# Turning memory rows before their norm is known, in a hybrid decoder step

## The reference, cut to what matters

```python
def rms_norm(x, g):
    y = xf * lax.rsqrt(jnp.mean(xf * xf, axis=-1, keepdims=True) + EPS)
    return (y * g.astype(jnp.float32)).astype(x.dtype)

def memory_kv(mem, p):            # mem (1, 256, 1024)
    mn = rms_norm(mem, p["g_mem"])
    mk = (mn @ p["w_mk"]).reshape(Bm, M, N_XHEADS, XHEAD_DIM)   # w_mk (1024, 1024)
    mv = (mn @ p["w_mv"]).reshape(Bm, M, N_XHEADS, XHEAD_DIM)
```

## Time and profile before

| | |
|---|---|
| median of 3 runs | 1738.87 us (1736.15 to 1744.55) |
| profiled execution | 1745.4 us, of which its span is 1743.6 us |
| PE busy | 1692.7 us, 97% |
| DVE, ACT busy | 1112.3 us (64%), 917.5 us (53%) |
| first instruction of PE | at 10.65 us |
| chain that ended last | PE 81%, DVE 6%, ACT 5%, DMA 4%, issue 3% |

### The profile page before, as it was taken

How to read it: one execution, slowest core, us unless ns; L and a number is a source line. 1 busy time by engine, 2 the same in 40 slices (tenths; PEclk the granted TensorE clock), 3 DMA queues, 4 the chain that set the end, 5 groups by cost and what they waited for, 6 DMA issues and landing times.

```text
span 1743.6 us, 29783 instructions
## 1 busy us (share of the span) xinstructions
PE 1692.7 (97%) x11750; PEld 1580.7 (91%) x11750; DVE 1112.3 (64%) x2055; ACT 917.5 (53%) x1675; POOL 2.2 (0%) x12
## 2 busy tenths in 40 slices
PE   7999999989999999999999999999999999999998
PEld 7999999845669999888779999999999999999998
DVE  5489998777665677435367767644676534676533
ACT  7534444755667676555456555444545433555433
POOL 0000000000000000000000000000000000000000
PEclk9999999989999999999999999999999999999999
DMA  8899967486215645443534344444445444445443
GB/s 279 202 246 217 234 176 162 155 313 237 86 56 157 186 145 159 148 131 109 162 117 122 109 131 134 131 134 142 137 135 157 139 137 143 135 134 154 139 138 100
DMA packets 400673, 271.45 MB, mean 156 GB/s; under 512 B 54252, under 2 KB 374882, under 8 KB 399184
## 3 DMA queue, kind: packets, MB, share of 16 engines
q1 hardware_dynamic: 395688, 260.72, 51.9%
q10 hardware_dynamic: 4847, 8.83, 1.5%
HBM read 225.40 MB, written 27.23 MB: 145 GB/s over the span
## 4 chain that ended last, share of the span: by engine, by line
PE 81%; DVE 6%; ACT 5%; DMA 4%; issue 3%; SPq 1%; ACTq 1%; DVEq 0%
PE bank L1345 76%; PE bank L1342 5%; DMA raw<-in_w_in_dram 2%; ACT whi L703 1%; ACT WORDS L824 1%; DMA raw<-in_w_mv_dram 1%; DVE C L1959 1%; ACT wide L717 1%; DVE Pp L1963 1%; DVE cv L1959 1%; DMA cached_t<-keys_turned 0%; DVE RSCF L2095 0%; ACTq L894 0%; SPq L537 0%; DMA out_dram<-KS 0%
## 5 line engine op out<-in xcount | busy, mean ns | idle before, releaser
L1345 PE MATMUL bank<-op_hi,whi 128*128 128x352 f32 x1632 | 539.6, 331 | 1.3 <-DVE wlo L1972 0.8
L1972 DVE TENSOR_TENSOR wlo<-raw,whi 128x1024 fp32r<-128x1024 f32 (+1 forms) x312 | 374.3, 1201 | 256.8 <-ACT whi L703 256.3
L1345 PE MATMUL bank<-op_hi,wlo 128*128 128x352 f32 x1632 | 526.4, 323 | 0.0
L1345 PE MATMUL bank<-op_lo,whi 128*128 128x352 f32 x1632 | 525.3, 322 | 0.0
L703 ACT ACTIVATE whi<-raw 128x1024 fp32r<-128x1024 f32 (+1 forms) x312 | 325.4, 1043 | 316.1 <-DMA raw<-in_w_down_dram 95.4
L1345 PEld LDWEIGHTS bank<-op_hi,whi 128*128 128x128 f32 x1632 | 307.7, 189 | 10.1 <-issue 7.0
L1345 PEld LDWEIGHTS bank<-op_lo,whi 128*128 128x128 f32 x1632 | 309.1, 189 | 0.6
L1345 PEld LDWEIGHTS bank<-op_hi,wlo 128*128 128x128 f32 x1632 | 307.6, 189 | 0.0
L1345 PE MATMUL bank<-fhi,whi 128*128 128x352 f32 x528 | 171.3, 324 | 0.0
L1345 PE MATMUL bank<-fhi,wlo 128*128 128x352 f32 x528 | 170.9, 324 | 0.0
L1345 PE MATMUL bank<-h1hi,whi 128*128 128x352 f32 x480 | 159.5, 332 | 3.3 <-DVE wlo L1972 3.3
(11 more groups left out here) (294 smaller groups left out, 2283.2 us busy)
## 6 DMA issues: line engine op xcount, KB each, us to landing
raw<-in_w_up_dram SPq DMA_DIRECT2D x132, 512.0 KB, 3.8
raw<-in_w_down_dram SPq DMA_DIRECT2D x48, 512.0 KB, 4.1
raw<-in_w_out_dram SPq DMA_DIRECT2D x24, 512.0 KB, 4.2
raw<-in_w_xq_dram SPq DMA_DIRECT2D x24, 512.0 KB, 4.2
raw<-in_w_xo_dram SPq DMA_DIRECT2D x24, 512.0 KB, 4.2
PLANES<-HALVES SPq DMA_DIRECT2D x96, 112.0 KB, 3.7
keys_turned<-WORDS SPq DMA_DIRECT2D x24, 448.0 KB, 3.1
cached_t<-keys_turned SPq DMA_DIRECT2D x6, 1792.0 KB, 9.6
```

Source lines behind the costliest of these rows:

```text
L1345: return pe.matmul(out, lhsT, rhs, start=first, stop=last, skip_group_check=shared)
L1972: dve.tensor_tensor(wlo[v % SLOTS][:, 0:nk, :], raw[v % SLOTS][:, 0:nk, :], whi[v % SLOTS][:, 0:nk, :].bitcast(F32), ALU.subtract).then_in ...
```

## The change

- `PRM` is put in another order: `g_mem` comes first, so its 8 rows are loaded first, with a semaphore of their own. PE turns those 8 rows alone; DVE copies them alone. The other 68 are turned behind key unit 0, through bank 4, and copied by DVE behind its `memory_unit(0)`.
- `DGM` is gone. PE turns the blocks of `mtk` by the plain identity as soon as the two tiles have landed; `mhi` and `mlo` carry the gain only.
- ACT's squares and root of the memory are moved behind `token_roots(0)`. DVE's reciprocal of them is moved behind `token_scales(0)`.
- The norm, one number per memory token, is applied where the rows leave the bank as token rows: `memory_rows` on DVE and on ACT now has two instructions of 128 x 128 with a scale by partition, in place of one copy of 128 x 256.
- ACT's `whi` of unit 0 and DVE's `wlo` of unit 0 stand in the middle of the eight `mhi` and `mlo`, not ahead of them.

```diff
-PRM = (("g_pre_mix", 8), ("g_out_attn", 4), ("g_out_conv", 4), ("g_post_mix", 8), ("g_pre_x", 8), ("g_mem", 8),
+PRM = (("g_mem", 8), ("g_pre_mix", 8), ("g_out_attn", 4), ("g_out_conv", 4), ("g_post_mix", 8), ("g_pre_x", 8),
        ("g_post_x", 8), ("g_pre_ffn", 8), ("g_post_ffn", 8), ("conv_b", 4), ("ln_conv_g", 4), ("ln_conv_b", 4))
...
         def memory_rows(t):
             m = MEM_UNITS[t][1]
             act.wait_ge(*at("mtk_t", t))
-            act.activation((MKO if t < NT else MVO)[:, :, m * P:(m + 1) * P], bank[7][:, 0:NM].rearrange("p (t n) -> p t n", t=MT), ACT.Copy).then_inc(*mark("mtok", t))
-
+            if t == NT - 1:
+                act.wait_ge(*at("xr", "m"))
+            for mt in range(MT):
+                ins = act.activation((MKO if t < NT else MVO)[:, mt, m * P:(m + 1) * P], bank[7][:, mt * P:(mt + 1) * P], ACT.Copy, scale=rx3[:, 9 + mt:10 + mt])
+            ins.then_inc(*mark("mtok", t))
+
+        act.wait_ge(*at("prm", "g_mem"))
+        for m in range(NT):
+            if m == NT // 2:
+                split_to(0)
+            act.wait_ge(*at("mt", m))
+            act.activation(mhi[:, m, :], bank[m % 6][:, 0:NM], ACT.Copy, scale=g_of("g_mem", m)).then_inc(*mark("mhi", m))
+        split_to(1)
+        token_roots(0)
         for i in range(MT):
             act.wait_ge(*at(f"mem_in{i}", 0))
             square_rows(mtk[i][:, :], 9 + i, P)
         act.wait_ge(*at("xss", 10))
         act.activation(rx2[:, 9:11], ssx[:, 9:11, 0], ACT.Sqrt, bias=eps[:, :], scale=1.0 / D).then_inc(*mark("msd", 0))
-        split_to(0)
         act.wait_ge(*at("prm", "gains"))
-        for m in range(NT):
-            act.wait_ge(*at("mt", m))
-            act.activation(mhi[:, m, :], bank[m % 6][:, 0:NM], ACT.Copy, scale=g_of("g_mem", m)).then_inc(*mark("mhi", m))
-        split_to(1)
-        token_roots(0)
         for t in range(NT):
             split_to(t + 2)
...
         pe.wait_ge(*at("ident", 0))
-        pe.wait_ge(*at("prm_in", PRM[-1][0]))
-        turn(bank[7][:, 0:PRM_N], stage_p[0:PRM_N, 0, :]).then_inc(*mark("prm_t", "gains"))
-        reader[7] = ("prm", "gains")
+        pe.wait_ge(*at("mem_gain", "g_mem"))
+        turn(bank[7][:, 0:NT], stage_p[0:NT, 0, :]).then_inc(*mark("prm_t", "g_mem"))
+        reader[7] = ("prm", "g_mem")
         for m in range(NT):
             take(m % 6, "mlo", m)
             for i in range(MT):
-                pe.wait_ge(*at("mn", i))
-                ins = mm(bank[m % 6][:, i * P:(i + 1) * P], mtk[i][:, m * P:(m + 1) * P], DGM[i][:, :], True, True)
+                pe.wait_ge(*at(f"mem_in{i}", 0))
+                ins = turn(bank[m % 6][:, i * P:(i + 1) * P], mtk[i][:, m * P:(m + 1) * P])
             ins.then_inc(*mark("mt", m))
...
         for t in range(NT):
             memory_unit(t, 7 - t % 2)
+            if t == 0:
+                pe.wait_ge(*at("prm_in", PRM[-1][0]))
+                take(4, "prm", "gains")
+                turn(bank[4][:, 0:PRM_N], stage_p[0:PRM_N, 0, :]).then_inc(*mark("prm_t", "gains"))
...
-        dve.wait_ge(*at("msd", 0))
-        dve.reciprocal(rx3[:, 9:11], rx2[:, 9:11]).then_inc(*mark("xr", "m"))
-        dve.wait_ge(*at("xr", "m"))
-        dve.wait_ge(*at("ident", 0))
-        for i in range(MT):
-            dve.tensor_scalar(DGM[i][:, :], ident[:, :], rx3[:, 9 + i:10 + i], None, ALU.mult).then_inc(*mark("mn", i))
-        dve.wait_ge(*at("prm_t", "gains"))
-        dve.tensor_copy(prm[:, :], bank[7][:, 0:PRM_N]).then_inc(*mark("prm", "gains"))
-        low_to(0)
+        dve.wait_ge(*at("prm_t", "g_mem"))
+        dve.tensor_copy(prm[:, 0:NT], bank[7][:, 0:NT]).then_inc(*mark("prm", "g_mem"))
         for m in range(NT):
+            if m == NT // 2:
+                low_to(0)
             dve.wait_ge(*at("mhi", m))
             stt(mlo[:, m, :], bank[m % 6][:, 0:NM], g_of("g_mem", m), mhi[:, m, :].bitcast(F32), ALU.mult, ALU.subtract).then_inc(*mark("mlo", m))
...
         def memory_rows(t, b):
             m = MEM_UNITS[t][1]
             dve.wait_ge(*at("mtk_t", t))
-            dve.tensor_copy(MKO[:, :, m * P:(m + 1) * P], bank[b][:, 0:NM].rearrange("p (t n) -> p t n", t=MT)).then_inc(*mark("mtd", t))
+            for mt in range(MT):
+                ins = dve.tensor_scalar(MKO[:, mt, m * P:(m + 1) * P], bank[b][:, mt * P:(mt + 1) * P], rx3[:, 9 + mt:10 + mt], None, ALU.mult)
+            ins.then_inc(*mark("mtd", t))
...
             if t == 0:
+                dve.wait_ge(*at("prm_t", "gains"))
+                dve.tensor_copy(prm[:, NT:PRM_N], bank[4][:, NT:PRM_N]).then_inc(*mark("prm", "gains"))
+                dve.wait_ge(*at("ident", 0))
                 token_scales(0)
+                dve.wait_ge(*at("msd", 0))
+                dve.reciprocal(rx3[:, 9:11], rx2[:, 9:11]).then_inc(*mark("xr", "m"))
+                dve.wait_ge(*at("xr", "m"))
```

More of the change, by code:

```diff
@@ L204, in layout @@
     DGX = [mn(f"DGX{i}", 124160 + 512 * i if i < TT else 132640, [P, P]) for i in range(TT + 1)]
-    DGM = [mn(f"DGM{i}", 133152 + 512 * i, [P, P]) for i in range(MT)]
     junk = mn("junk", 157920, [P, 512])
@@ L707, in _ @@
         for n, k in PRM:
[L708 removed]
+            act.dma_start(stage_p[r:r + k, 0, :], A[n].rearrange("a (k p) -> (a k) p", p=P)).then_inc(*mark("mem_gain" if n == "g_mem" else "prm_in", n, 16))
             r += k
```

3 lines of the change are left out of this document (1 added, 2 removed).

## The result

| | runs | median us | range |
|---|---|---|---|
| kernel before | 20 | 1740.56 | 1736.15 to 1747.1 |
| kernel after | 20 | 1744.28 | 1740.21 to 1747.69 |

The ratio is 1.0018, 95% interval [1.0010, 1.0026]: the change makes the kernel slower by about 3 us, where the forecast was a gain of 0.1 us. The profiled execution of the kernel after took 1745.63 us, span 1743.8, against a span of 1743.6 before. Two single profiles therefore don't show the loss as a longer span; it has to be looked for by stretches, and in more than one profile of each kernel.

The account below looks back on a forecast made before the run. PE is busy 97% of the span, so only its start could win, set by the wait ending at 37.72 us. -0.17 + 0.1 = -0.1 us on the median 1738.87 gave 1738.8 us, range 1734.0 to 1744.5.

Parts of the forecast that it names:

- What bounds the start: PE's start: its last wait, ended at 37.72 us, goes back through DVE and ACT to the landings of units.
- the sum: Wait that ended at 37.72 us: -0.17 on ACT plus 0.1 on DVE gives -0.1 us, ending near 37.6.
- The head start: Start: unit 0 5.8 us earlier, all gone at `whi` of unit 3; rival that it passes: 3.8 us won, chance 0.08.
- The scaled pair: DVE's `memory_rows` at 35.46: two scaled instructions for one copy, +0.03 to +0.16 us, taken as +0.1.
- `whi` of unit 3: ACT at the start: between -0.06 and +0.09 us against 25.11, taken as +0.04.
- The clock: TensorE's first rows are slow, 0.205 us each; rival that the slow stretch begins with unit 2: +1.4 us, chance 0.08.
- Slow work in unit 0: PE's start: unit 0 would take 5.1 us for 3.0 and end at 16.4, before unit 1 at 17.9.
- all of unit 0 would run slow: PE's start: by the skill's rule transposes don't count as activity for the clock; not in the sum.
- Later stalls fall otherwise: Rival: the long stalls of 3.34 and 3.71 us, one gone or doubled, about 5 us; chance 0.05 each.
- The base: Whole kernel: the median of three runs, 1738.87 us, on which the sum of 0.1 us is put.

Follow-up runs that it names:

- a3_loads: Kernel after, memory's squares and root moved ahead of `whi` of unit 1, activations' loads issued one step later between the weights': 1739.86 us, ratio 0.9999.
- c_after: Kernel after once more, unchanged, against the kernel before: 1743.60 us, ratio 1.0019.
- b5_late6: Kernel before with six tiny chained square roots on ACT ahead of the second token group's squares: 1743.65 us, ratio 1.0016.
- a1: Kernel after without the norm of the memory tokens, rows leaving the bank in one plain copy: 1743.22 us, ratio 1.0009.
- a2: Kernel after with the memory's squares and root moved ahead of `whi` of unit 1, into ACT's idle time: 1743.27 us, ratio 1.0011.
- c_before: Kernel before once more, unchanged, against itself: 1741.20 us, ratio 1.0004.
- a7_pad15: a3_loads with 15 small transposes ahead of PE's first work: 1738.24 us, ratio 0.9985.
- c_a7: a7_pad15 once more, unchanged, against the kernel before: 1738.99 us, ratio 0.9986.
- b6: Kernel before with 113 small transposes ahead of PE's first work: 1746.02 us, ratio 1.0027.
- a8: a7_pad15 with 79 small transposes in place of 15: 1739.41 us, ratio 0.9984 against the kernel before.
- b1_tworows: Kernel before with its rows leaving the bank in two instructions scaled by 1, in place of one copy: 1743.23 us, ratio 1.0013.
- b2_late: Kernel before with two tiny chained square roots on ACT ahead of the second token group's squares: 1743.45 us, ratio 1.0009.
- b7_pad64: Kernel before with 64 small transposes ahead of PE's first work: 1741.15 us, ratio 0.9996.
- c_a3: a3_loads once more, unchanged, against the kernel before: 1742.99 us, ratio 1.0011.

## Why the prediction was wrong, step by step

**What bounds the start** was right. That unit 0 would move to 11.3 (11.37), that ACT would then wait for the landing of unit 1 until 15.5 (15.70), unit 1 run at 17.9 (18.07), the squares stand at 21.6 (21.76) and unit 2 start at 26.6 (26.89), all came as the sum had it, within 0.3 us. The head start did die at unit 3. a3_loads shows the reason from the other side: with the loads in another order part of it gets through.

**One term of the sum was mis-sized, and one scatters.** The scaled pair cost 0.19 us against the copy (0.18 in c_after) and not 0.1. `whi` of unit 3 came at 25.68, 0.57 us later than before and not 0.04; but in c_after it stands at 25.07, without a wait, which is the forecast, and in b5_late6, whose start is that of the kernel before up to there, at 25.65 behind a wait of 1.03 us. So this landing differs by 0.6 us from one execution to the next, and the 0.57 can't be put down to the change. The start as a whole is +0.43 us in this profile where -0.1 stood (38.15 against a forecast of 37.6, which c_after meets with 37.53); over the four kernels with after's plain start (after, c_after, a1, a2) it ends at 37.75 on the mean, against 37.51 for before and c_before: +0.2 us. The start alone would have been a result of no difference, a little on the slow side.

**The clock.** The prediction read the 0.205 us of the `DGM` rows as a slow clock, and it was right, though the stretch view of the kernel before prints 1.00:

```profile
10.80:14.00 3.20, 3.20 (x16) 1.00 1.09 361
```

Slow work in unit 0, the case that the prediction weighed, came in the second profile of the kernel after. PE's timeline of c_after:

```profile
11.19 0.55 PE L1350 MATMUL bank<-mhi,whi 128*128 128x256 f32 x1 [1.11 <-issue]
11.54 0.42 PE L1350 MATMUL bank<-mlo,whi 128*128 128x256 f32 x1
...
16.17 0.28 PE L1350 MATMUL bank<-mhi,wlo 128*128 128x256 f32 x1
16.29 0.23 PE L1347 MATMUL bank<-ident,stage_p 76*128 76x76 f32 x1
17.77 0.38 PE L1350 MATMUL bank<-mhi,whi 128*128 128x256 f32 x1 [1.25 <-DVE wlo L1981]
```

Unit 0 takes 5.1 us there, as forecast for this case, and ends before unit 1 is ready; nothing further on moves. In the first profile unit 1 was the slow one: its token blocks came 1.4 us later than in c_after (23.70 against 22.30, where 0.7 was foreseen), and unit 2 only 0.3. By the rule of the Trainium skill that was weighed there ("TensorE: Matmul & The Clock Gate", "Part 4: PE-mode transpose") all of unit 0 would run slow behind turns alone. The traces are divided: in four of the eleven profiles with these turns unit 0 runs at half speed until 14.5 to 16.1 us (c_after, a3_loads, a7_pad15, c_a7), in the other seven the records begin at 10.0 to 11.1 us with 1.00, when PE had done nothing but turns, and unit 0 runs at full speed. As a rule without exception it doesn't hold here.

**The step that failed** is "Later stalls fall otherwise ... A shift of 0.1 us gives no reason for either", by which the stalls behind the start entered the sum with nothing. What the runs showed in its place is a stretch from unit 9 to unit 25 that is 2.3 us longer on the mean (124.9 against 122.6). The mechanism was named, how SP's key stream meets the rest, and its place, the stall at 138 us. But only a shift of the start was looked at as its trigger, and by that it was given 0.05. The change had a second way into this stretch, which the runs show for a part of the 2.3 us: it shortened PE's program by 30 instructions, and so moved every load of PE's code against SP's key stream. The page of before showed the queue `q8 instruction`, and the earlier trace rows the 32 `DGM` records; the prediction costed these as time on PE and as nothing else.

**How much is settled.** Shown: the place of the code load at 88 or 92 us switches SP's pattern in both kernels, and that piece is 0.75 us longer with after's place. Likely, as the ranges overlap: the first part of the stretch, unit 9 to 17, is 64.2 us on the mean of the seven kernels with after's code, 63.2 for before's six, and 62.6 for the three with 15 transposes, but 63.8 in b6 and 63.7 in a8. Shown as a time: the transposes take 2.6 ± 0.6 us off a3_loads; for the kernel after itself, 0.9 ± 0.6, it is only likely.

Not settled: the second part of the stretch, unit 17 to 25, is 1.3 us longer with after's code and 0.9 with b1_tworows, where only DVE's and ACT's programs grew, and 0.8 without any scaled row (a1). The `q14 instruction` packets, perhaps code of these engines, move too (one at 158.0 us in b1 and 160.1 in c_after, none between 107 and 183 in before). But a1 has none between 107 and 185 either and still loses its 0.8 us, and no run moved them alone. Nor is it known where b6_pad113 lost its other 3 us, or why 0.33 us of delay (b2_late) cost 2.5 ± 0.6; its roots also lengthen ACT's program, so it is not a delay alone, and b7_pad64, whose start ends at 38.00 us like that of b2_late, costs +0.4 ± 0.6.

Against these losses 0.9 us come back between units 33 and 35 (24.7 us on the mean with after's code, 25.6 with before's). So the profiles account for 0.2 + 2.3 - 0.9 = 1.6 us of the 2.9 ± 0.4 that the runs measured, and behind unit 35 they show no loss (1443.9 us to the end on the mean with after's code, 1444.6 with before's, single profiles 1441.8 to 1447.8). The rest has no place.

**A rival that no run tests** is the granted clock later on. The record lists it for 175 runs of the kernel before: from 0.989 to 0.996, and a run is 1.5 us longer for each 0.001 less (correlation -0.82). Most of the spread between single runs goes with it. b6_pad113 was granted 0.9912 on the mean of its runs, the kernel before 0.9931; by that slope, an estimate, this is 2.9 of its 5.0 us. For the kernel after (0.9911 and, in c_after, 0.9927) the shares can't be set off so, since the 6.8 us at half speed in unit 1 lower the share of its first profile by 0.002 and cost nothing. Longer stalls may bring more time at half speed behind them, or the half speed may fall otherwise for another reason; the runs don't separate the two.

**The base** was off as well: 1738.87 was the median of three runs, and all 195 have a mean of 1741.1. That is 2.2 us of the 5.5 between forecast and result, and no step of the argument; the upper end of 1744.5 just held it.

## What to carry to other kernels

An edit that gives an engine fewer or more instructions also moves every later load of that engine's code; where a queue of dependent transfers sets the pace, look up in the instruction queues of the transfer view where these loads fall, before a loss of some microseconds is put down to the edit's own work. To test it, give the instructions back as work on nothing in idle time. Repeat it on more than one kernel: here the same 15 transposes gave 2.6 ± 0.6 us in one and 0.9 ± 0.6 in another. And a head start that ends in a wait for a landing has to be won in the order of the loads: with the squares moved alone (a2_fill) the start ended at 37.80 us, with the loads reordered too at 36.54 and 35.21 (a3_loads, c_a3), though of that no time was left against before (+0.5 ± 0.5).
